# Matrix products that walk their columns backwards in blocks of sixteen

## The chip, the cores and the metric

One core of a Trainium2 chip runs the kernel. The metric is device time in microseconds (us); the kernel before takes 2259.56 us, the median of three runs (2258.78 to 2261.01).

## The reference

The reference is two transformer-like blocks in float32 over 256 tokens with 2048 features, with 256 context tokens beside them in the first. Cut to the parts that carry weights:

```
# first block
mod    = silu(c) @ w_mod + b_mod                    # 2048 -> 6 x 2048, also for c_ctx
hx, hc = modulate(rms_norm(x)), modulate(rms_norm(ctx))
z      = h @ w_in                                   # queries, two gates, values, and the rest
o      = hgrn2_chunk_scan(...)                      # both directions, state from the context
merged = sigmoid(ga) * (y_a @ w_pa) + sigmoid(gb) * (y_b @ w_pb)
x      = x + g1 * (merged @ w_o)
a, b   = split(modulate(rms_norm(x)) @ w_up, 2)     # 2 x 5632 columns
x      = x + g2 * ((silu(dwconv_grid(a)) * b) @ w_down)
# second block, on 16 meta tokens and the 256 tokens
proj   = rms_norm_2(h) @ w_in_2                     # eight parts of 1024 columns
mixed  = [stick-breaking attention, differential attention], gated
y      = mixed @ w_out_2
return (h + y)[:, N_META:]
```

Nearly all the work is products of an activation matrix of 256, 272 or 512 (tokens and context) columns with weights that are read once each.

## The kernel before, in words

Everything is kept features by tokens: 128 features on the partitions, tokens along the free axis. A product makes 128 output features: for each of its 16 (in "down": 11 per quarter) blocks of 128 input features it multiplies a 128x128 block of weights with 128 x T activations, and all of them add up in one bank of PSUM (`ACC`, four banks taken in turn).

For float32 accuracy, weights and activations are each split into a high and a low part of the type fp32r. ScalarE copies the weights that have landed in `RAW` to `HI` (line 488), VectorE writes the rest, raw minus high, to `LO` (line 1308), both in half products of 128 x 1024 values. TensorE then issues three matmuls for each block: high weights by high activations, high weights by low activations, low weights by high activations. Each matmul has its own load of 128 columns of weights (the LDWEIGHTS of the trace), which runs beside the matmul before it. All products go through `prod` (line 878) except the first three of "rec" (`early_step`, line 930) and the first two of "up" (`up_step`, line 1135), and all matmuls through `mm` at line 876.

The activations that stream through the array are `HX` (phases rec, mix and merge; in rec the token and the context stream are read by one matmul of 2 x 256 columns), `YAB` (merge), `MRG` (out), `HXU` (up), `SH` and `SL` (down), `U2` (attn: 272 columns where the 16 meta tokens take part, 256 where they don't) and `MIX` (proj). The core of `prod`, and the two-stream operand of rec:

```
o = out(k)
mm(o, HI[:, slot, k, 0:P], xh(k), start=first, stop=False)
mm(o, HI[:, slot, k, 0:P], xl(k), start=False, stop=False)
ins = mm(o, LO[:, slot, k, 0:P], xh(k), start=False, stop=last)

xch, xcl = (lambda k: HX[:, 0:3:2, k, 0:T]), (lambda k: HX[:, 1:4:2, k, 0:T])
```

The phases follow each other in the order mod1, rec, mix, merge, out, up, down, attn, proj, each a loop that is the same on all engines. Between the products stand TensorE's small matmuls of the recurrence (`mix_level` and others) and of the attention, into four other banks (`AUX`). SyncE fetches a weight block of 1 MB for every product into one of the four slots of `RAW`, as soon as VectorE has made the low part out of the block that was there. Order is kept by semaphores: `lo_half` says that half a product's weights are split, `mm_half` that half a product is computed, `bank_free` that a bank has been read.

In `HX`, `HXU`, `MRG`, `YAB`, `SH`, `SL` and `MIX` the 256 columns of one block lie beside each other, 1024 bytes on each partition; in `U2` a block has 320 columns, of which 272 are used. The two streams of `HX` lie 32 KB apart.

Of the kernel before, what the change touches and what calls it, by code (L numbers as in the profile page):

```python
# [14 lines left out]
P = 128  # L15
D = 2048
KD = D // P
T = 256
# [113 lines left out]
def build(nc, xct, metat, crow, vec, con1, con2, wts, wdown, park, outt):  # L132
    ctx = ExitStack()
    with ctx:
        base = 8320

        def at(name, kb, shape, dt=F32):
            return nc.alloc_sbuf_tensor_at(name, shape, dt, offset=base + int(kb * 1024))
# [6 lines left out]
        HI = at("hi", 32, [P, 2, 16, P], F32R)  # L145
        LO = at("lo", 49, [P, 2, 16, P], F32R)
# [19 lines left out]
        HXU = at("hxu", 66.1875, [P, 2, KD, T], F32R)  # L166
# [101 lines left out]
        ACC = ctx.enter_context(nc.psum_tensor("acc", [P, 4, 512], F32))  # L268
# [70 lines left out]
        def prod_index(ph, i, p):  # L339

            k = KINDS[ph]
            n = p - k[:p].count("m")
            return PROD0[ph] + i * (len(k) - k.count("m")) + n
# [5 lines left out]
        def used(ph, i, p):  # L349

            return 2 * (unit(ph, i, p)[0] - UNIT0["rec0"])

        def halves(ph):
            return ((0, DH), (DH, DT)) if ph == "down" else ((0, 8), (8, 16))
# [517 lines left out]
        def _(pe):  # L872
            for one in (kd_tr, v_tr, s_mm, o_mm, ss2_mm, ss3_mm, d_sc, dv_tr, d_av, b_z, bv_tr, b_av):
                pe.sem_inc(one, 1)
            def mm(*a, **k):
                return pe.matmul(*a, **k)  # L876

            def prod(ph, i, p, xh, xl, out, groups=None, bank_wait=None, between=None,
                     lo_at=None, inputs=None, each=1, needs=None):


                q, slot = prod_index(ph, i, p), prod_index(ph, 0, p) % 2
                if bank_wait is None:
                    pe.wait_ge(bank_free, q - 3)
                elif bank_wait is not False:
                    pe.wait_ge(bank_free, bank_wait)
                n = halves(ph)[1][1]
                for h, (a, b) in enumerate(halves(ph)):
                    if h and between:
                        between()  # L890
                    pe.wait_ge(lo_half, (used(ph, i, p) if lo_at is None else lo_at) + h + 1)
                    for k in range(a, b):
                        if needs and k in needs:
                            pe.wait_ge(inputs, needs[k])
                        elif inputs and not needs and k % 4 == 0:
                            pe.wait_ge(inputs, each * (k // 4 + 1))
                        first, last = groups(k) if groups else (k == 0, k == n - 1)
                        o = out(k)
                        mm(o, HI[:, slot, k, 0:P], xh(k), start=first, stop=False)
                        mm(o, HI[:, slot, k, 0:P], xl(k), start=False, stop=False)  # L900
                        ins = mm(o, LO[:, slot, k, 0:P], xh(k), start=False, stop=last)
                    ins.then_inc(mm_half, 1)

            def rows(i, p):
# [19 lines left out]
            xch, xcl = (lambda k: HX[:, 0:3:2, k, 0:T]), (lambda k: HX[:, 1:4:2, k, 0:T])  # L924
# [5 lines left out]
            def early_step(s, k, high, low):  # L930

                if k % 8 == 0:
                    pe.wait_ge(lo_half, 2 * s + k // 8 + 1)
                o = ACC[:, s, :].rearrange("p (s t) -> p s t", s=2)
                mm(o, high, xch(k), start=k == 0, stop=False)
                mm(o, high, xcl(k), start=False, stop=False)
                ins = mm(o, low, xch(k), start=False, stop=k == KD - 1)
                if k == KD - 1:
                    ins.then_inc(mm_half, 2)

# [23 lines left out]
            for k in range(KD - LAG, KD):  # L964
                early_step(2, k, HIV[:, k, :], LOV[:, k, :])

            def rec_turns(i):

                pe.wait_ge(kd_ready, i + 1)
                pe.wait_ge(kdt_ready, 1 + i)  # L970
                for d in range(2):
                    for t in range(2):
                        ins = pe.transpose(AUX[:, 0, (2 * d + t) * P:(2 * d + t + 1) * P], EXC[:, d, t * P:(t + 1) * P], c1("ident"))  # L973
                ins.then_inc(kd_tr, 1)
                pe.wait_ge(bank_free, prod_index("rec", i, 4) + 1)
                pe.wait_ge(vt_ready, 1 + i)
                for s in range(2):
                    for t in range(2):
                        ins = pe.transpose(AUX[:, 1, (2 * s + t) * P:(2 * s + t + 1) * P], VS[:, s, t * P:(t + 1) * P], c1("ident"))  # L979
                ins.then_inc(v_tr, 1)  # L980

            def rec_state(i):

                pe.wait_ge(kdt_ready, 1 + i + 1)
                pe.wait_ge(vt_ready, 1 + i + 1)
                pe.wait_ge(s_ready, 1 + i)
                for d in range(2):
                    for t in range(2):
                        ins = mm(AUX[:, 2, d * P:(d + 1) * P], KDT[:, 2 * d + t, :], VCT[:, t, :], start=t == 0, stop=t == 1)
                ins.then_inc(s_mm, 1)  # L990

            def rec_query(ph, i, p, between=None):

                prod(ph, i, p, lambda k: HX[:, 0, k, 0:T], lambda k: HX[:, 1, k, 0:T], lambda k: ACC[:, 3, 0:T],
                     between=between)
# [6 lines left out]
            def rec_head(i, second=False):  # L1002

                for p in range(3):
                    prod("rec", i, 2 * p, xch, xcl, lambda k: ACC[:, p, :].rearrange("p (s t) -> p s t", s=2),
                         between=first_turns if second and p == 0 else None)
                    if second and p == 0:
                        rec_state(0)
                rec_query("rec", i, 6, lambda: rec_turns(i))
                rec_state(i)  # L1010
# [51 lines left out]
            def mix_head(i, peeled):  # L1062

                xh, xl = (lambda k: HX[:, 0, k, 0:T]), (lambda k: HX[:, 1, k, 0:T])

                prod("mix", i, 0, xh, xl, lambda k: ACC[:, 0, 0:T], between=None if peeled else lambda: mix_level(i - 1, 7))
                if peeled:
                    pe.wait_ge(s_ready, 1 + HEADS)
                else:
                    mix_outputs(i - 1)  # L1070
                mix_same(i)
                mix_level(i, 0)
                prod("mix", i, 1, xh, xl, lambda k: ACC[:, 1, 0:T], between=lambda: mix_level(i, 1))
                if not peeled:
                    mix_turn(i - 1)
                mix_level(i, 2)
                prod("mix", i, 2, xh, xl, lambda k: ACC[:, 2, 0:T], between=lambda: mix_level(i, 3))
                mix_level(i, 4)
                prod("mix", i, 3, xh, xl, lambda k: ACC[:, 3, 0:T], between=lambda: mix_level(i, 5))
                mix_level(i, 6)  # L1080
# [54 lines left out]
            def up_step(p, k):  # L1135

                slot = prod_index("up", 0, p) % 2
                if k % 8 == 0:
                    pe.wait_ge(lo_half, used("up", 0, p) + k // 8 + 1)
                o = ACC[:, p, 0:T]  # L1140
                mm(o, HI[:, slot, k, 0:P], HXU[:, 0, k, 0:T], start=k == 0, stop=False)
                mm(o, HI[:, slot, k, 0:P], HXU[:, 1, k, 0:T], start=False, stop=False)
                return mm(o, LO[:, slot, k, 0:P], HXU[:, 0, k, 0:T], start=False, stop=k == KD - 1)

            pe.wait_ge(bank_free, prod_index("up", 0, 1) - 3)
            for n in range(KD + BEHIND):
                if n < KD:
# [4 lines left out]
                    ins = up_step(0, n)  # L1152
                    if n % 8 == 7:
                        ins.then_inc(mm_half, 1)
                if n >= BEHIND:
                    ins = up_step(1, n - BEHIND)
# [11 lines left out]
            with pe.Fori(0, ITERS["down"]) as i:  # L1168
                for jj in range(2):
                    for q in range(4):  # L1170
                        p = 4 * jj + q
                        u = prod_index("down", i, p)
                        if jj == 0:
# [3 lines left out]
                             bank_wait=u - 4 if q == 0 else False)  # L1177
# [13 lines left out]
            def attn_head(i, peeled):  # L1191

                def proj(p, meta, between=None, inputs=None, needs=None, bank_wait=None):

                    a = 0 if meta else NMETA
                    prod("attn", i, p, lambda k: U2[:, 0, k, a:TA], lambda k: U2[:, 1, k, a:TA],
                         lambda k: ACC[:, p % 4, 0:TA - a], between=between, inputs=inputs, needs=needs,
                         bank_wait=bank_wait)

                def tokens_major(src, bank):  # L1200

# [4 lines left out]
                if peeled:  # L1206
                    proj(0, False, between=last_squares, inputs=u2_ready, needs={k: k + 1 for k in range(KD)},
                         bank_wait=PROD0["attn"] - 4)
# [22 lines left out]
                for c in range(2):  # L1231
                    r = slice(64 * c, 64 * c + 64)
                    mm(AUX[:, c, 0:P + NMETA], DQK[r, 0, NMETA:NMETA + P], DQK[r, 1, 0:P + NMETA], start=True, stop=True)
                    ins = mm(AUX[:, c, P + NMETA:P + NMETA + TA], DQK[r, 0, NMETA + P:TA], DQK[r, 1, :], start=True, stop=True)
# [4 lines left out]
                for key, (a, q, w) in enumerate(SBQ):  # L1239
                    ins = mm(AUX[:, 1, a:a + w], SKF[:, key * P:(key + 1) * P], SQF[:, q:q + w], start=True, stop=True)  # L1240
# [44 lines left out]
            with pe.Fori(0, ITERS["proj"]) as i:  # L1285
                for p in range(4):
                    prod("proj", i, p, lambda k: MIX[:, 0, k, 0:T], lambda k: MIX[:, 1, k, 0:T], lambda k: ACC[:, p, 0:T],
                         inputs=mix_ready, needs=head_order if p == 0 else {KD: 0})
# [789 lines left out]
```

## Time and profile before

| | |
|---|---|
| median of three runs | 2259.56 us |
| profiled execution, span from first to last instruction | 2259.2 us |
| TensorE, matmuls | 2223.9 us, 98% |
| TensorE, weight loads | 2143.9 us, 95% |
| VectorE | 1633.3 us, 72% |
| ScalarE | 995.8 us, 44% |
| DMA | 475.73 MB, 211 GB/s on average |

For the profiled execution there is the span alone, and it lies 0.4 us under the median of the runs. A matmul's duration in the trace runs from its start to the end of its pipeline, so neighbours overlap; what tells the pace is the distance from one start to the next, or a stretch divided by the matmuls in it. "PE" rows are matmuls and "PEld" rows weight loads. One row of the windows view gives a stretch of time and for each engine its busy time and the number of instructions.

### The profile page before, as it was taken

What the parts mean: (1) busy time and instruction counts of PE and PEld (TensorE: products, weight loads), DVE (VectorE), ACT (ScalarE), POOL (GpSimd) and SP (SyncE); (2) the same over time, 40 slices, a digit from 0 to 9 for tenths busy, and PEclk for the clock granted to TensorE, in tenths of its full rate; (3) what the DMA queues carried; (4) which work ended last, traced back from release to release, by engine and by line L of the source; (5) the groups of instructions that cost most, each with busy time, mean ns of one, the idle gap of its engine ahead of it and who ended that gap; (6) DMA issues with size and microseconds to landing.
All of it is one profiled execution on the core that took longest, in us unless ns stands there. A gap on an engine that the chain in (4) does not pass through costs nothing.

```text
span 2259.2 us, 48355 instructions
## 1 busy us (share of the span) xinstructions
PE 2223.9 (98%) x18451; PEld 2143.9 (95%) x18451; DVE 1633.3 (72%) x2523; ACT 995.8 (44%) x1402; POOL 8.4 (0%) x18
## 2 busy tenths in 40 slices
PE   5999999999999999999999999999999999999999
PEld 4788888999999999999999999999999999999999
DVE  4465565899987666998888888875656766767764
ACT  4332222565543333454444444444445444444453
POOL 0000000000000000000000000000000000000000
PEclk8999999999999999999999999999999999999999
DMA  9955565444468766894555555556556444444443
GB/s 404 401 228 206 197 233 191 168 149 149 149 225 312 284 257 239 339 354 169 200 192 199 188 186 198 194 211 202 189 185 233 150 152 165 149 154 162 149 177 139
DMA packets 69519, 475.73 MB, mean 211 GB/s; under 512 B 7728, under 2 KB 9776, under 8 KB 18384
## 3 DMA queue, kind: packets, MB, share of 16 engines
q1 hardware_dynamic: 68688, 467.59, 56.1%
q0 software_dynamic: 768, 7.26, 0.9%
q8 instruction: 44, 0.72, 0.1%
q14 instruction: 19, 0.16, 0.0%
HBM read 469.58 MB, written 5.24 MB: 210 GB/s over the span
## 4 chain that ended last, share of the span: by engine, by line
PE 93%; DMA 4%; DVE 2%; ACT 1%; issue 0%; SPq 0%; DVEq 0%; ACTq 0%
PE acc L876 87%; PE aux L876 5%; DMA raw<-wts 4%; DVE lo L1308 1%; PE aux L1203 0%; DVE cv L1744 0%; DVE n L1688 0%; ACT hi L488 0%; PE aux L979 0%; PE aux L973 0%; DVE raw L1318 0%; DVE u L1772 0%; PE aux L1250 0%; DVE hxu L1325 0%; PE aux L1252 0%
## 5 line engine op out<-in xcount | busy, mean ns | idle before, releaser
L1308 DVE TENSOR_TENSOR lo<-raw,hi 128x1024 fp32r<-128x1024 f32 (+1 forms) x714 | 810.0, 1168 | 185.0 <-ACT hi L488 180.3
L488 ACT ACTIVATE hi<-raw 128x1024 fp32r<-128x1024 f32 (+1 forms) x714 | 693.8, 1012 | 299.9 <-PE acc L876 235.2
L876 PE MATMUL acc<-hx,hi 128*128 128x256 f32 (+1 forms) x3040 | 648.4, 311 | 1.3 <-DVE hx L1371 1.3
L876 PEld LDWEIGHTS acc<-hx,hi 128*128 128x128 f32 x3040 | 488.8, 189 | 37.1 <-issue 2.4
L876 PE MATMUL acc<-hxu,hi 128*128 128x256 f32 x2816 | 479.8, 276 | 0.5 <-DVE lo L1308 0.3
L876 PE MATMUL acc<-hx,lo 128*128 128x256 f32 (+1 forms) x1520 | 468.1, 308 | 0.0
L876 PEld LDWEIGHTS acc<-hxu,hi 128*128 128x128 f32 x2816 | 424.1, 188 | 1.6 <-DVE hxu L1325 1.1
L876 PE MATMUL acc<-hxu,lo 128*128 128x256 f32 x1408 | 388.7, 276 | 0.0
L876 PE MATMUL acc<-u,hi 128*128 128x272 f32 (+1 forms) x2048 | 381.6, 288 | 0.0
L876 PEld LDWEIGHTS acc<-u,hi 128*128 128x128 f32 x2048 | 318.1, 189 | 4.3 <-issue 2.5
L876 PEld LDWEIGHTS acc<-hx,lo 128*128 128x128 f32 x1520 | 287.9, 189 | 16.7
L876 PE MATMUL acc<-u,lo 128*128 128x256 f32 (+1 forms) x1024 | 291.1, 284 | 0.0
L876 PEld LDWEIGHTS acc<-hxu,lo 128*128 128x128 f32 x1408 | 264.3, 188 | 0.0
L876 PE MATMUL acc<-sh,hi 128*128 128x256 f32 x704 | 194.3, 276 | 0.0
L876 PE MATMUL acc<-sl,hi 128*128 128x256 f32 x704 | 194.3, 276 | 0.0
L876 PE MATMUL acc<-sh,lo 128*128 128x256 f32 x704 | 194.3, 276 | 0.0
L876 PEld LDWEIGHTS acc<-u,lo 128*128 128x128 f32 x1024 | 192.7, 188 | 0.0
L876 PEld LDWEIGHTS acc<-sh,hi 128*128 128x128 f32 x704 | 132.2, 188 | 0.0
L876 PEld LDWEIGHTS acc<-sl,hi 128*128 128x128 f32 x704 | 132.2, 188 | 0.0
L876 PEld LDWEIGHTS acc<-sh,lo 128*128 128x128 f32 x704 | 132.2, 188 | 0.0
L1744 DVE SCALAR_TENSOR_TENSOR cv<-at,vec,cv 128x256 f32<-128x256 f32 x308 | 129.5, 480 | 0.0
L876 PE MATMUL acc<-yab,hi 128*128 128x256 f32 x512 | 91.2, 281 | 0.3 <-DVE lo L1308 0.3
(301 smaller groups left out, 2327.0 us busy)
## 6 DMA issues: line engine op xcount, KB each, us to landing
raw<-wts SPq DMA_DIRECT2D x389, 1024.0 KB, 4.8
raw<-wdown SPq DMA_DIRECT2D x64, 704.0 KB, 4.1
xc<-xct SPq DMA_DIRECT2D x1, 4096.0 KB, 12.6
rawx<-wts SPq DMA_DIRECT2D x2, 1024.0 KB, 24.3
x<-xct SPq DMA_DIRECT2D x1, 2048.0 KB, 11.1
park<-x POOLq DMA_DIRECT2D x1, 2048.0 KB, 9.6
xf<-park POOLq DMA_DIRECT2D x1, 2048.0 KB, 9.0
outt<-outs SPq DMA_DIRECT2D x16, 128.0 KB, 3.4
```

Source lines behind the costliest of these rows:

```text
L488: A.activation(HI[:, slot, a:b, 0:P], RAW[:, p % 4, a:b, :], ACT.Copy).then_inc(hi_half, 1)
L876: return pe.matmul(*a, **k)
L1308: V.tensor_tensor(LO[:, slot, a:b, 0:P], RAW[:, p % 4, a:b, :], HI[:, slot, a:b, 0:P].bitcast(F32), ALU.subtract).then_inc(lo_half, 1)
L1744: mark(V.scalar_tensor_tensor(acc4[n % 2], a, w, acc4[n % 2], ALU.mult, ALU.add))
```

## The change

Each operand of the products, the columns read and the columns written in PSUM, gets an access pattern with another order. `paired` takes 256 columns as two halves of eight blocks of 16 and goes through them from the last block to the first, in each step first the block of the first half and then that of the second: columns 112 to 127, 240 to 255, 96 to 111, 224 to 239, and so on. `streams` does it with the two streams of rec: columns 240 to 255 of the one, 240 to 255 of the other, 224 to 239 of the one, and so on. Inside a block the columns ascend. The result of a column goes to the place where it went before. The products with 272 columns keep their order. Number, size and operands of the matmuls, waits, loads and all other engines' instructions stay as they are.

```
+            def paired(x):
+                return x.rearrange("p (b a c) -> p a b c", b=2, c=16)[:, ::-1]
+
+            def streams(x):
+                return x.rearrange("p s (a c) -> p a s c", c=16)[:, ::-1]
...
             def prod(ph, i, p, xh, xl, out, groups=None, bank_wait=None, between=None,
-                     lo_at=None, inputs=None, each=1, needs=None):
+                     lo_at=None, inputs=None, each=1, needs=None, order=paired):
...
-                        o = out(k)
-                        mm(o, HI[:, slot, k, 0:P], xh(k), start=first, stop=False)
-                        mm(o, HI[:, slot, k, 0:P], xl(k), start=False, stop=False)
-                        ins = mm(o, LO[:, slot, k, 0:P], xh(k), start=False, stop=last)
+                        o, high, low = order(out(k)), order(xh(k)), order(xl(k))
+                        mm(o, HI[:, slot, k, 0:P], high, start=first, stop=False)
+                        mm(o, HI[:, slot, k, 0:P], low, start=False, stop=False)
+                        ins = mm(o, LO[:, slot, k, 0:P], high, start=False, stop=last)
...
-                o = ACC[:, s, :].rearrange("p (s t) -> p s t", s=2)
-                mm(o, high, xch(k), start=k == 0, stop=False)
+                o = streams(ACC[:, s, :].rearrange("p (s t) -> p s t", s=2))
+                mm(o, high, streams(xch(k)), start=k == 0, stop=False)
...
                     prod("rec", i, 2 * p, xch, xcl, lambda k: ACC[:, p, :].rearrange("p (s t) -> p s t", s=2),
-                         between=first_turns if second and p == 0 else None)
+                         between=first_turns if second and p == 0 else None, order=streams)
...
-                o = ACC[:, p, 0:T]
-                mm(o, HI[:, slot, k, 0:P], HXU[:, 0, k, 0:T], start=k == 0, stop=False)
+                o, high, low = (paired(x) for x in (ACC[:, p, 0:T], HXU[:, 0, k, 0:T], HXU[:, 1, k, 0:T]))
+                mm(o, HI[:, slot, k, 0:P], high, start=k == 0, stop=False)
...
                          lambda k: ACC[:, p % 4, 0:TA - a], between=between, inputs=inputs, needs=needs,
-                         bank_wait=bank_wait)
+                         bank_wait=bank_wait, order=(lambda x: x) if meta else paired)
```

## Rows read from the trace of the kernel before

**Rows 1.** The page: busy time, share of the span and instructions of each engine.
```profile
PE 2223.9 (98%) x18451; PEld 2143.9 (95%) x18451; DVE 1633.3 (72%) x2523; ACT 995.8 (44%) x1402; POOL 8.4 (0%) x18
```
**Rows 2.** What TensorE waited for: us in total, times, longest.
```profile
PE aux L876 <- DMA raw<-wts: 21.4, 7, 16.5
PE acc L876 <- DMA raw<-wts: 7.1, 5, 4.9
```
**Rows 3.** Stretches in mix, merge, out, up, down, attn, proj: busy (instructions), clock, DMA share, GB/s.
```profile
core 0: us, PE busy (x) PEld busy (x) DVE busy (x) ACT busy (x) POOL busy (x), PEclk, DMA share, GB/s
410.00:650.00 240.00, 239.80 (x2069) 238.71 (x2068) 224.28 (x388) 141.04 (x247) 4.74 (x9) 1.00 0.43 157
660.00:900.00 240.00, 240.00 (x2040) 240.00 (x2040) 168.13 (x198) 93.69 (x112) 0.00 (x0) 1.00 0.74 280
930.00:990.00 60.00, 59.65 (x506) 59.45 (x505) 56.77 (x66) 26.63 (x33) 0.00 (x0) 1.00 0.99 386
1010.00:1490.00 480.00, 479.45 (x4217) 478.40 (x4217) 406.64 (x703) 228.34 (x317) 0.00 (x0) 1.00 0.53 189
1500.00:1730.00 230.00, 230.00 (x2032) 230.00 (x2031) 135.32 (x175) 107.33 (x153) 0.00 (x0) 1.00 0.61 206
1740.00:2160.00 420.00, 419.89 (x3366) 410.05 (x3366) 294.35 (x495) 198.66 (x289) 0.00 (x0) 1.00 0.43 155
2175.00:2255.00 80.00, 80.00 (x709) 80.00 (x708) 38.75 (x44) 28.73 (x27) 0.00 (x0) 1.00 0.47 169
```
**Rows 4.** Ten microseconds of merge, the same columns.
```profile
700.00:710.00 10.00, 10.00 (x88) 10.00 (x87) 9.17 (x11) 4.44 (x5) 0.00 (x0) 1.00 0.98 366
```
**Rows 5.** Groups of product matmuls, whole span: count, busy us, mean ns of one.
```profile
L876 PE MATMUL acc<-hxu,hi 128*128 128x256 f32 x2816 | 479.8, 276 | 0.5 <-DVE lo L1308 0.3
L876 PE MATMUL acc<-hx,hi 128*128 128x256 f32 x2304 | 414.0, 283 | 0.0
L876 PE MATMUL acc<-hx,hi 128*128 128x512 f32 x736 | 234.4, 400 | 1.3 <-DVE hx L1371 1.3
L876 PE MATMUL acc<-sh,hi 128*128 128x256 f32 x704 | 194.3, 276 | 0.0
L876 PE MATMUL acc<-u,hi 128*128 128x256 f32 x1024 | 185.1, 284 | 0.0
L876 PE MATMUL acc<-u,lo 128*128 128x256 f32 x512 | 142.8, 279 | 0.0
```
**Rows 6.** The third of each block's matmuls in mix and in merge.
```profile
L876 PE MATMUL acc<-hx,lo 128*128 128x256 f32 x543 | 151.3, 279 | 0.0
...
L876 PE MATMUL acc<-hx,lo 128*128 128x256 f32 x456 | 128.1, 281 | 0.0
```
**Rows 7.** Order of time, TensorE in rec: start us, us from there.
```profile
340.38 0.40 PE L876 MATMUL acc<-hx,lo 128*128 128x512 f32 x1
340.61 0.63 PE L876 MATMUL acc<-hx,hi 128*128 128x512 f32 x2
341.08 0.39 PE L876 MATMUL acc<-hx,lo 128*128 128x512 f32 x1
```
**Rows 8.** Order of time, small matmuls in mix, then in attn.
```profile
421.65 0.60 PE L876 MATMUL aux<-qla 128*128 128x128 f32 x4
...
1783.02 0.86 PE L876 MATMUL aux<-lz,con 128*128 128x416 f32 x2
1783.72 0.55 PE L876 MATMUL aux<-lz,onep 128*128 128x144 f32 x4
```
**Rows 9.** Waits in out (930 to 990 us), then in up (1100 to 1300 us).
```profile
ACT hi L488 <- DMA raw<-wts: 4.2, 9, 1.5
...
DVE cv L1730 <- ACT cv L754: 23.9, 18, 1.4
```

More of the change, by code:

```diff
@@ L933, in early_step @@
                     pe.wait_ge(lo_half, 2 * s + k // 8 + 1)
-                o = ACC[:, s, :].rearrange("p (s t) -> p s t", s=2)
-                mm(o, high, xch(k), start=k == 0, stop=False)
-                mm(o, high, xcl(k), start=False, stop=False)
-                ins = mm(o, low, xch(k), start=False, stop=k == KD - 1)
+                o = streams(ACC[:, s, :].rearrange("p (s t) -> p s t", s=2))
+                mm(o, high, streams(xch(k)), start=k == 0, stop=False)
+                mm(o, high, streams(xcl(k)), start=False, stop=False)
+                ins = mm(o, low, streams(xch(k)), start=False, stop=k == KD - 1)
                 if k == KD - 1:
@@ L1139, in up_step @@
                     pe.wait_ge(lo_half, used("up", 0, p) + k // 8 + 1)
-                o = ACC[:, p, 0:T]
-                mm(o, HI[:, slot, k, 0:P], HXU[:, 0, k, 0:T], start=k == 0, stop=False)
-                mm(o, HI[:, slot, k, 0:P], HXU[:, 1, k, 0:T], start=False, stop=False)
-                return mm(o, LO[:, slot, k, 0:P], HXU[:, 0, k, 0:T], start=False, stop=k == KD - 1)
+                o, high, low = (paired(x) for x in (ACC[:, p, 0:T], HXU[:, 0, k, 0:T], HXU[:, 1, k, 0:T]))
+                mm(o, HI[:, slot, k, 0:P], high, start=k == 0, stop=False)
+                mm(o, HI[:, slot, k, 0:P], low, start=False, stop=False)
+                return mm(o, LO[:, slot, k, 0:P], high, start=False, stop=k == KD - 1)
             pe.wait_ge(bank_free, prod_index("up", 0, 1) - 3)
```

## The prediction

> **What bounds the kernel now.** I read the busy line first: TensorE's matmuls fill 98% of the span [rows 1]. Then what TensorE waits for: 28.5 us for weights from DMA [rows 2], nearly all at the start, where nothing is changed (the slices of the page show the empty stretch there); all else together is under 4 us. So from the start of rec on, TensorE is the bound, and the time is the number of product matmuls times the distance from one to the next. Last I read that distance, stage by stage, out of stretches that hold nothing but products [rows 3]:
>
> - up 480/4217 = 113.8 ns and down 230/2032 = 113.2 ns; proj the same within its edges (80/709 = 112.8). I take 113.3 for all three.
> - merge 240/2040 = 117.6 ns; out 60/506 = 118.6 with 0.35 us idle, I take 117.6 as well.
> - rec, 512 columns: three matmuls in 341.08 - 340.38 = 0.70 us, 233 ns each [rows 7].
> - mix and attn mix both paces. A matmul at the slow pace lasts 281 ns (merge), at the fast one 276 (down) [rows 5, 6]; mix with 279 lies three fifths of the way up, near 116 ns. The 256-column matmuls of attn have 279 and 284 in their two groups [rows 5], where the first of a product counts longer, so again near 116.
>
> All of them run at a granted clock of 1.00, the level of 2.4 GHz. At one column per cycle 256 columns would need 106.7 ns and 512 columns 213.3. So each product matmul has an excess: 6.6 ns at the fast pace, 10.9 at the slow one, 20 with 512 columns.
>
> **Where the excess comes from decides everything.** Three things in the rows:
>
> 1. Merge and up have the same shapes and the same kind of operands, and yet two paces, each held for hundreds of microseconds [rows 3]. So at least 4.3 ns is no fixed cost of a matmul.
> 2. It is not the traffic of others: in ten microseconds of merge with the DMA engines 98% busy the pace is 88 matmuls in 10 us, just as over the whole stage at 74% [rows 3, 4], and down with VectorE at 59% runs as up at 85% [rows 3]. What is left is TensorE against itself: columns streaming in while the next weights load beside them (x2040 of both in 240 us).
> 3. The small matmuls show what a fixed cost can be. Four of 128 columns last 0.60 us in all, so with 0.275 for the last they start (0.60 - 0.275)/3 = 0.108 us apart, each with its own weights. Two of 416 columns start (1783.72 - 1783.02)/2 = 0.35 us apart [rows 8]; at half rate, two cycles a column, which fits, that is 346.7 ns and an excess of some 3. So where the columns come at half the rate, beside the same weight loads, excess is 1 to 3 ns.
>
> My reading: of the excess, 2 to 3 ns is fixed, and the rest is the full-rate column reads and the weight reads getting in each other's way in SBUF. How often they do depends on how their addresses run against each other, which explains why one shape can have two paces. The change alters just that: columns now go downwards through memory, and every 128 columns' worth of addresses takes as long as a load of 128 weight columns does. If weight loads walk from the last column to the first, the two move together and never meet. That direction no row shows, and it is the weak point.
>
> The Trainium skill ("TensorE: Matmul & The Clock Gate", Single matmul latency and Back-to-back issue gap) gives columns/2.4 + 2.5 ns for the distance of warm matmuls; that would be 109.2 and 215.8 here, and the trace is 4 to 18 ns above it. By this page alone the sum below is the same within 3 us.
>
> **The change part by part.** It adds no instruction, no byte and no wait. If the meetings go, I take 109 ns for 256 columns: a matmul can't follow faster than its weights, and 0.108 is the closest that any pair of load and matmul comes [rows 8]. For 512 columns 213.3 + 2.4 = 215.7. Counts are from the groups [rows 5]; with the third matmul they are half as many again as the group of high weights.
>
> - up 2816 x 1.5 = 4224, at 4.3 ns: 18.2 us
> - down 3 x 704 = 2112, at 4.3: 9.1 us
> - proj 4 blocks of four products of 48 = 768, at 4.3: 3.3 us
> - rec, 512 columns: 736 x 1.5 + 48 of the early third product = 1152, at 17.6: 20.3 us
> - rec, eight query products, 384 at about 7: 2.7 us
> - mix 4 x 8 x 48 = 1536 at 7: 10.8 us
> - merge, 48 products, 2304 at 8.6: 19.8 us
> - out 16 x 48 = 768 at 8.6: 6.6 us
> - attn, four products of a head without the meta tokens, 1024 x 1.5 = 1536 at 7: 10.8 us
> - attn with 272 columns, 1536: order unchanged, nothing.
>
> Sum 101.6 us. What is late next takes some back:
>
> - Out: DMA is 99% busy at 386 GB/s, and ScalarE already waits 4.2 us for weights [rows 3, 9]. Eight blocks of 1.05 MB per four products ask for 8.4 MB / 22.6 us = 371 GB/s now and 401 at the new pace. I leave 2 of the 6.6 us.
> - Mix: VectorE is busy 224 of 240 us [rows 3], and the stage would shrink to 230 with a chain of small matmuls in it. I leave half, 5.4.
> - Up: VectorE busy 407 of 480 us; it also waits 23.9 of 200 us for ScalarE's copy of a finished bank [rows 9], 1.3 us in each pair of products. That wait follows on the product's end, so it is slack, and 0.9 us of it is left when a pair takes 10.5 instead of 10.9. Nothing lost.
> - Merge (VectorE 70%, DMA 280 GB/s, 302 after), down, attn, proj: covered. One microsecond for chains in attn.
>
> 101.6 - 4.6 - 5.4 - 1 = 90.6, so 2259.2 - 90.6 = 2168.6 in the profiled execution, whose span is 0.4 us under the median: 2169 us.
>
> What the pattern itself costs, no row shows: 15 jumps in a matmul of 256 columns, 31 in one of 512. The nearest row is the 512-column matmul, which jumps once between two streams: 233 against twice 113.3 (excess 6.4 ns) or twice 117.6 (saving 2.2) [rows 3, 7]. So a jump lies between -2 and +6 ns. I take nothing, since 117.6 is the pace of the same tile HX. The upper end would be 13,632 x 15 x 6 ns, over a millisecond, and I hold it for very unlikely. The other rule against the change is in the Trainium skill ("SBUF — State Buffer", Door 1: The DMA port swizzle): any PSUM pattern that isn't contiguous slows matmuls significantly, PSUM having lines of 8 bytes. Runs of 64 bytes fill whole lines, so by the mechanism it names the cost would be nothing, by its letter it would be rival 3.
>
> **Rivals.**
>
> 1. *Only the slow pace goes.* The 113.3 has some other cause (a fixed cost at full rate), and only the meetings beyond it vanish. Then mix 1536 x 2.7, rec's queries 384 x 2.7, merge 2304 x 4.3, attn 1536 x 2.7, out nothing, and 512 columns 233.3 to 2 x 113.3 = 226.7, 1152 x 6.6: 4.1 + 1.0 + 9.9 + 4.1 + 7.6 = 27, to 2232 us. For it: 113.3 is steady over 900 us of three stages with different tiles. Against: the small matmuls' 1 to 3 ns.
> 2. *The order doesn't matter.* The excess depends on when a weight load starts, not on addresses: 2259.6, within 3 us. For it: the two paces appear with like tiles. The Trainium skill says ("TensorE: Matmul & The Clock Gate", Step-by-step: what each phase is for) that TensorE has two independent SBUF read ports and that loading weights takes no bandwidth from the running matmul; by it the columns' order could not matter, and the excess that the rows show would be left as it is.
> 3. *Every jump costs TensorE cycles*, on the read or the write. There are 13,632 x 15 + 1152 x 31 = 240,000 jumps. One cycle of 0.42 ns each is 100 us and just eats the whole gain of 102: that is the point from which it decides. Two cycles, with the meetings gone, give 2259 - 102 + 200 = 2357 us; one cycle without any gain 2360. For it: no product of this kernel has ever more than one jump. Against: the two-stream matmul of rec, with a jump, takes less than two of merge without one. A variant on the same side: weights are read upwards, and more meetings come than before; at one more of 6.6 ns in each matmul about +90 us.
>
> **Chances.** Forecast 0.50 (own range 2155 to 2200). Rival 1 0.14 (2215 to 2245). Rival 2 0.10. Rival 3 0.26, of which 0.08 lies near the break-even point, between 2264 and 2290, and the rest above. Faster by over 0.2% 0.64, within 0.2% (4.5 us, what runs of this kernel can tell) 0.10, slower 0.26. The range from 2150 to 2285 leaves out the costly part of rival 3, 0.18, and little below.
>
> **What would show it.** Right: down, up and proj at 109 ns (a stretch of 230 us with some 2110 instructions), merge at 109 too, one pace instead of two, 512 columns at 216, the mean of one near 272; TensorE still 98% busy; more idle time of TensorE in out, ended by the split of weights or DMA. Rival 1: 113.3 everywhere and 276 ns. Rival 2: both paces in the same places. Rival 3: product matmuls over 118 ns, 272-column ones in attn as long as now. My forecast is wrong if 256-column products still start 113 ns or more apart in down.

## The result: slower, and one pace in place of two

The changed kernel takes 2286.93 us, the median of four runs (2285.32 to 2287.49), against 2259.17 for the kernel before (2249.98 to 2261.01): ratio 1.0132, interval 1.0108 to 1.0156. Forecast were 2169 us in a range from 2150 to 2285, and slower with a chance of 0.26. The profiled execution has a span of 2285.5 us, 26.3 more than before. The kernel before does not always take the same time: one of its four runs here lies near 2250, and experiment 7 comes back to that.

The page after, TensorE and its waits, beside [rows 1, 2]:

```profile
PE 2247.8 (98%) x18451; PEld 2174.1 (95%) x18451; DVE 1633.1 (71%) x2523; ACT 995.5 (44%) x1402; POOL 8.4 (0%) x18
```
```profile
PE aux L876 <- DMA raw<-wts: 23.0, 8, 17.2
PE acc L876 <- DMA raw<-wts: 8.9, 7, 3.8
```

The stages after, as in [rows 3, 4] (each stage begins a little later, so attn and proj are taken 20 us later):

```profile
core 0: us, PE busy (x) PEld busy (x) DVE busy (x) ACT busy (x) POOL busy (x), PEclk, DMA share, GB/s
410.00:650.00 240.00, 239.87 (x2055) 239.25 (x2054) 223.32 (x386) 141.15 (x246) 4.21 (x8) 1.00 0.43 153
660.00:900.00 240.00, 240.00 (x2048) 240.00 (x2047) 166.74 (x194) 95.53 (x115) 0.00 (x0) 1.00 0.76 281
930.00:990.00 60.00, 59.77 (x510) 59.57 (x509) 56.62 (x67) 26.43 (x33) 0.00 (x0) 1.00 0.98 378
1010.00:1490.00 480.00, 479.90 (x4087) 479.63 (x4087) 393.82 (x682) 218.43 (x300) 0.00 (x0) 1.00 0.51 183
1500.00:1730.00 230.00, 230.00 (x1962) 230.00 (x1961) 133.16 (x174) 99.91 (x136) 1.70 (x2) 1.00 0.57 194
1760.00:2180.00 420.00, 419.89 (x3344) 410.08 (x3343) 291.95 (x491) 197.48 (x288) 0.00 (x0) 1.00 0.43 154
2195.00:2275.00 80.00, 80.00 (x684) 80.00 (x683) 41.07 (x47) 30.75 (x30) 0.00 (x0) 1.00 0.49 167
```

Divide stretch by matmuls (a row also counts the two or three that lie only partly in the stretch, which matters in short stretches): up 480/4087 = 117.4 ns, down 230/1962 = 117.2, proj 117.0, merge 240/2048 = 117.2, out 117.6. Where there were 113.3 and 117.7 there is one pace now, 117.3, and it is nearly the slow one. Rec alone gained, beside [rows 7]: three matmuls in 341.32 - 340.64 = 0.68 us, 226.7 ns instead of 233.3.

```profile
340.64 0.39 PE L876 MATMUL acc<-hx,lo 128*128 128x512 f32 x1
340.87 0.61 PE L876 MATMUL acc<-hx,hi 128*128 128x512 f32 x2
341.32 0.39 PE L876 MATMUL acc<-hx,lo 128*128 128x512 f32 x1
```

The groups say the same in durations, beside [rows 5]: 276 has become 280 in up, and 400 has become 393 in rec.

```profile
L876 PE MATMUL acc<-hxu,hi 128*128 128x256 f32 x2816 | 496.4, 280 | 0.2
L876 PE MATMUL acc<-hx,hi 128*128 128x512 f32 x736 | 229.9, 393 | 1.4 <-DVE hx L1379 1.4
```

The account: up, down and proj 7104 x 4.0 = +28.4 us; mix 2069 x (116.8 - 116.0) = +1.7; attn 3366 x (125.6 - 124.8) = +2.7; merge and out 3072 x -0.3 = -0.9; rec 1152 x -6.67 = -7.7; waits for the first weights +3.4. Together +27.6, measured +26.3.

### The profile page after: what moved, and what is told of

Its sections match the earlier page's. It is cut to its first block, busy times and chain, and to the rows that moved or that the text cites. A ratio compares the mean times of both kernels' runs of the same rounds, so it can differ in the third digit from the quotient of the medians.

```text
span 2285.5 us, 48355 instructions
## 1 busy us (share of the span) xinstructions
PE 2247.8 (98%) x18451; PEld 2174.1 (95%) x18451; DVE 1633.1 (71%) x2523; ACT 995.5 (44%) x1402; POOL 8.4 (0%) x18
## 4 chain that ended last, share of the span: by engine, by line
PE 93%; DMA 4%; DVE 1%; issue 0%; ACT 0%; SPq 0%; DVEq 0%; ACTq 0%
PE acc L876 88%; PE aux L876 5%; DMA raw<-wts 4%; DVE lo L1316 0%; PE aux L1211 0%; DVE n L1696 0%; PE aux L981 0%; PE aux L987 0%; DVE raw L1326 0%; DVE u L1780 0%; ACT hi L488 0%; PE aux L1258 0%; DVE hxu L1333 0%; SPq L374 0%; PE aux L1067 0%
## 5 line engine op out<-in xcount | busy, mean ns | idle before, releaser
L876 PE MATMUL acc<-hxu,hi 128*128 128x256 f32 x2816 | 496.4, 280 | 0.2
L876 PEld LDWEIGHTS acc<-hxu,hi 128*128 128x128 f32 x2816 | 429.8, 188 | 0.9 <-DVE hxu L1333 0.8
L876 PE MATMUL acc<-hxu,lo 128*128 128x256 f32 x1408 | 393.7, 280 | 0.0
## 6 DMA issues: line engine op xcount, KB each, us to landing
xc<-xct SPq DMA_DIRECT2D x1, 4096.0 KB, 13.4
```

## The experiments

In the edits `-` is the changed kernel unless said otherwise. "Pace" is the distance from one matmul's start to the next. In the runs with TensorE alone it is the mean over the second half of a case or more, worked out from the start times in the trace. "First column" or "at 48" is the place of the columns against the weights, in columns of 4 bytes, within the 512 bytes that one block of weights takes on a partition; in the kernel it is 48 for most tiles. The runs of a changed version were taken beside the kernel before, and their ratios are to it; only `rec_only` and `paired_only` ran beside each other, as did `near_weights` and `ahead56`, `low_moved` and `low_moved_rec`.

**1. The change in rec alone** (`rec_only`) and **in the 256-column products alone** (`paired_only`).

```
# rec_only
-                     lo_at=None, inputs=None, each=1, needs=None, order=paired):
+                     lo_at=None, inputs=None, each=1, needs=None, order=lambda x: x):
...
# paired_only, in streams(x)
-                return x.rearrange("p s (a c) -> p a s c", c=16)[:, ::-1]
+                return x
```

> The change in the two-stream products of rec alone; all 256-column products read plainly as before. Theory A (each form of product has its own pace, set by its own reading order): 1152 matmuls of 512 columns at 226.7 ns instead of 233.3, 7.7 us faster than before, about 2251; 256-column stages as before (113.3 in up, down and proj, 117.6 in merge and out). Rival L (the pace of a stage is carried over from what ran ahead of it, so that rec's order decides the pace of the later stages too): up and down at another pace than 113.3 although their order is the old one.

Measured: 2252.27 us, the median of ten runs, ratio 0.9977 (0.9959 to 0.9995), span 2250.2. Six runs lie at 2251 to 2253, one at 2244 and three near 2280. Rec gained its 7.7 us, and merge and down kept their paces, as theory A has it. But out, whose instructions and order are those of the kernel before, ran at 113.3: 443 matmuls in this stretch, where the kernel before has 422. And up began at 117.8 and changed to 113.3 after some 30 us. So theory A holds for rec only; a stage can change its pace although nothing in it was changed, which is on the side of rival L.

```profile
935.00:985.00 50.00, 50.00 (x443) 50.00 (x443) 49.16 (x57) 22.31 (x28) 0.00 (x0) 1.00 0.98 391
```

> The change in the 256-column products alone; rec's two-stream products read plainly. Theory A: 117.3 ns in every 256-column product, 233.3 in rec, so 7.7 us slower than the whole change, about 2295. Rival L: the 256-column stages go back to 113.3 and 117.6, about 2259.

Measured: 2309.41, ratio 1.0236 (1.0210 to 1.0263). Both numbers missed. Merge has 117.2, but up 480/4003 = 119.9 and down 230/1919 = 119.9:

```profile
660.00:900.00 240.00, 240.00 (x2048) 240.00 (x2047) 169.00 (x200) 94.66 (x113) 0.00 (x0) 1.00 0.75 280
1030.00:1510.00 480.00, 480.00 (x4003) 480.00 (x4002) 384.95 (x672) 212.71 (x293) 0.00 (x0) 1.00 0.51 182
1530.00:1760.00 230.00, 230.00 (x1919) 230.00 (x1918) 125.69 (x158) 96.33 (x130) 0.00 (x0) 1.00 0.58 191
```

So the parts don't add up: in the kernel the paired order has two paces at the same addresses, 117.4 and 120.0. Which one out, up and down get differs between this kernel and the changed one, though only rec's order, earlier on, differs; merge, between them, has 117.4 in both. By start times the 120.0 begins in out and ends in attn, and proj has 117.4 again.

**2. TensorE alone** (`bench1`): weights loaded beside columns as in the kernel, no other engine busy.

> Products alone, not the reference's computation: only TensorE works, with 96 matmuls for each of some 60 cases, as in the kernel two blocks of weights (high, low) in turn against two tiles of columns. The cases differ in the order in which columns are read and written, in the first column (which moves the columns' addresses against the weights' in steps of 64 bytes), in the number of columns, and in what ran ahead. With nothing else on the chip's memories, the plain order at the kernel's distance of 48 columns should give 113.3 or 117.8 ns if the excess is TensorE's own (every theory here), about 109 if it comes from other engines. Theory M (columns and weights meet in SBUF): pace depends on the first column, in some order reaches about 109; only the reading order counts, so reading paired and writing plainly gives 117.3, reading plainly and writing paired 113.3 or 117.8. Theory J (a jump costs time): paired, paired upwards and blocks from the end are alike at any first column, 8-column blocks (31 jumps) cost twice as much over the floor as 16, 32-column blocks half. Theory P (PSUM): writing paired and reading plainly gives 117.3, the reverse 113.3. The plain cases after fillers of different length show two paces if the pace depends on the start.

Four cases at the kernel's distance of 48 columns, eight microseconds of each: plain, paired, read paired and written plainly, read plainly and written paired. The counts include the two or three matmuls that reach in from outside, so the pace is not 8 us divided by them; 70 or 71 stand for some 117 to 118 ns, 73 for 113.

```profile
core 0: us, PE busy (x) PEld busy (x) ACT busy (x) POOL busy (x), PEclk, DMA share, GB/s
82.00:90.00 8.00, 8.00 (x70) 8.00 (x69) 0.00 (x0) 0.00 (x0) 1.00 0.00 0
173.50:181.50 8.00, 8.00 (x71) 8.00 (x70) 0.00 (x0) 0.00 (x0) 1.00 0.00 0
406.00:414.00 8.00, 8.00 (x70) 8.00 (x69) 0.00 (x0) 0.00 (x0) 1.00 0.01 2
417.00:425.00 8.00, 8.00 (x73) 8.00 (x72) 0.00 (x0) 0.00 (x0) 1.00 0.00 0
```

By start times, in ns:

```
first column          0      16     32     48     64     80     96     112
plain                 120.0  117.8  120.0  117.8  120.0  117.8  120.0  117.8
paired                121.4  113.3  116.7  117.4  120.8  116.7  116.7  117.4
paired, upwards       120.0         120.0         120.0         120.0
blocks from the end   117.8         120.0         117.8         120.0
                        first column 0    first column 48
read paired, write plain    120.7             117.4
read plain, write paired    120.0             113.3
halves swapped (1 jump)     120.0             117.8
paired in eights (31 jumps) 133.3             120.0
paired in 32s (7 jumps)     120.0             118.6
two streams: plain          226.7             233.4
two streams: down as changed 233.4            226.7
two streams: up             240.0             240.0
plain at 48 after matmuls of 24, 40, 56, 72, 104, 136 columns: 117.8 117.8 113.3 117.8 113.3 117.8
plain at 48 by columns: 128 to 224: 111.7;  240: 113.3;  272: 123.3;  288: 133.4;  320: 146.7
```

Four things follow. The excess is TensorE's own: 113.3, 117.8, 117.4, 226.7 and 233.4 come up with nothing else running. It is made on the reading side: reading paired gives the paired pace however it is written, and writing paired leaves plain's two paces (113.3 is one of them). Jumps between blocks of 16 columns have no cost of their own: paired at 16, with 15 of them, runs at 113.3, the lowest pace that any order has. Shorter blocks may cost: in eights, with 31 jumps, the pace is 13 ns over plain at one place and 2 at another. The place of the columns against the weights counts, as theory M said: at 0 the two-stream products are faster plain (226.7) than downwards (233.4), at 48 it is the other way round. But nothing reaches 109.

**3. Starts, places and widths** (`bench2`).

> Products alone again, not the reference's computation: TensorE only, 48 matmuls a case, 96 cases. What the first such run left open: (1) Is the excess tied to the weight load or to the columns? With 352 to 512 columns in one run of addresses a weight load covers less and less of a matmul: theory W (each weight load costs the column reads a few stretches of 16 columns) expects a constant excess of 13 to 20 ns over columns / 2.4, theory C (reading at full rate costs one part in sixteen) expects 6.25%, 9 ns at 352 and 13 ns at 512. (2) Is the pace of an order its own or does it depend on the start? Paired at distances 0, 16 and 48 after eight fillers: theory S (start matters only for the plain order, which crosses the weights; paired moves along with them) expects one pace per distance, 113.3 at 16 and 117.4 at 48; rival T expects two or more paces as for the plain order. (3) Is there an order or distance at 109? If columns and weights that move together could keep clear of each other, one of the eight distances of the two-stream order should reach 216 and one of the paired ones 109; if the least cost of a weight load is one stretch of 16 columns, nothing falls under 113.3 and 220.

```
plain at 48, columns:       352    384    416    448    480    512
pace                        160.0  173.4  186.7  202.3  216.1  233.3
over columns / 2.4           13.4   13.4   13.4   15.6   16.1   20.0
paired at 0, eight starts:   120.7 to 120.9
paired at 16, eight starts:  113.3 twice, 116.5 to 116.7 six times
paired at 48, eight starts:  117.0 to 117.6
two streams down, eight first columns: 233.2 228.3 228.4 226.7 233.2 228.3 228.4 226.7
```

From 352 to 416 columns the excess stands at 13.4 ns (and 13.4 at 320): it does not grow with the columns as theory C has it, which speaks for theory W, though at 448 to 512 it grows. Every matmul here has a weight load of its own, so a fixed cost of the matmul is not told apart from one of the load. Paired at 48 has one pace within 0.6 ns, at 16 two. Of the 96 cases none is under 113.3, nor under 226.6 with 512 columns.

**4. The starting matmul** (`bench3`).

> Products alone, not the reference's computation: TensorE only, plain order at the kernel's distance of 48 columns, 48 matmuls a case, each after one matmul of 8 to 256 columns; first one after another, then each from a case that followed a matmul of 56 columns. Theory S: both paces come up, 113.3 and 117.8, each steady within its case, by the length of the matmul ahead. If the pace before also matters, the two sweeps differ. At the end the paired order after 16 to 256 columns: 117.3 for all if its pace does not hang on the start, or 120.0 in some, as it had in up and down when rec ran plainly.

Plain after matmuls of 8 to 256 columns: 113.3 in 12 of 32 cases, 117.8 in 20, nothing between. With another case in front of each, the lengths that give 113.3 are partly others: 88 gave it only in the first sweep, 80 only in the second, and 56, repeated 32 times, gives now the one pace and now the other. So the length ahead does not choose the pace alone; what else does, within the exact timing of the start, no run shows. Paired: 117.0 to 117.6 in all 16; the 120.0 of `paired_only` did not come up.

**5. In the kernel: the place of the weights, and a matmul ahead** (`near_weights`, `ahead56`).

```
# near_weights
-        HI = at("hi", 32, [P, 2, 16, P], F32R)
-        LO = at("lo", 49, [P, 2, 16, P], F32R)
+        HI = at("hi", 32.125, [P, 2, 16, P], F32R)
+        LO = at("lo", 49.125, [P, 2, 16, P], F32R)
...
# ahead56, against rec_only, in prod
+                        if ahead and k == 0:
+                            mm(o[:, 0:ahead], HI[:, slot, k, 0:P], high[:, 0:ahead], start=True, stop=True)
```

> The changed kernel with the weight tiles HI and LO moved up by 128 bytes, so that the columns of HX, HXU, SH, MRG, YAB and MIX stand 16 columns from the weights' place in a 512-byte row instead of 48; nothing else differs. Theory M (how addresses of columns and weights stand to each other sets the pace): in TensorE's run alone, paired order at 16 had two paces, 113.3 and 116.7, and 117.3 at 48; so up, down (its low tile at another distance), proj and merge at 113 to 117, rec's 512 columns at 228 to 233 instead of 226.7; in all 2287 - 13632 x 0.7 to 4.0 + 1152 x 2 to 6.7, that is 2240 to 2285. Rival J (15 jumps cost a fixed time, wherever the tiles lie): 117.3 in all stages, 2287.

Measured: 2274.34, ratio 1.0063 (1.0028 to 1.0098): nearly 13 us less than the changed kernel by nothing but the tiles' addresses. Theory M; a fixed price of a jump would have left 2287. Up runs at 480/4114 = 116.7:

```profile
1010.00:1490.00 480.00, 480.00 (x4114) 479.75 (x4113) 395.47 (x688) 218.18 (x300) 0.00 (x0) 1.00 0.52 184
```

> The change in rec's two-stream products alone, all others plain, and one matmul of 56 columns more ahead of the first product of every round of merge and of out (nine in all), written where the product overwrites it. Theory S (the plain order has two paces at the same addresses, held from how the stream of matmuls started; a short matmul ahead can switch it): merge and out switch from 117.8 to 113.3, 3072 x 4.4 = 13.5 us less than with rec's change alone, about 2238. Rival U (the pace belongs to the stage: its tiles, its DMA traffic): merge and out stay at 117.8, 2252.

Measured: 2250.83, ratio 1.0006 (0.9959 to 1.0052), not the 2238 expected. The pace did switch within merge, but not as wished: one stretch came to 113.3 by start times (20 us with 178 matmuls, those at its edges included), another stayed slow (40 us with 342):

```profile
660.00:700.00 40.00, 40.00 (x342) 40.00 (x342) 34.43 (x38) 15.63 (x19) 0.00 (x0) 1.00 0.92 341
770.00:790.00 20.00, 20.00 (x178) 20.00 (x178) 14.31 (x20) 7.75 (x9) 0.00 (x0) 1.00 0.70 260
```

That both paces stand in one stage with one code speaks against rival U. The kernel before shows it too: its out is at 117.8 but for some 5 us from 924 us on, at 113.3. As a remedy the matmul ahead failed, and experiment 4 shows why: after 56 columns either pace can come. Nor was 2238 the right mark, since out was fast in `rec_only` already.

**6. An order or a place with one good pace** (`bench4`).

> Products alone, not the reference's computation: TensorE only, 48 matmuls a case, in search of an order with one pace at 113.3 from every start. Eight reading orders at distances 16 and 48, each after matmuls of 8, 32, 48 and 96 columns; the plain order with the low weights moved by 64, 128 and 256 bytes; the plain order at distances that split the 64-byte stretches. Theory S (where column and weight reads meet is a matter of phase, and an order can offer one stable phase or several): each order has its own set of one or two paces; the plain one 113.3 and 117.8 by start, and at least one other may have 113.3 alone. Rival R (113.3 is only ever one of two phases): every order that shows 113.3 after one start shows 117 or more after another. Orders with 3, 7 or 15 jumps have the plain paces among theirs if a jump is free.

```
after matmuls of             8      32     48     96 columns
plain, 48                    113.3  117.8  117.8  113.3
blocks of 64, 48             113.4  117.8  117.7  113.4
blocks of 32, 16             117.8  117.7  113.3  113.3
blocks of 16, 16             120.0  120.0  120.0  120.0
plain, low weights + 64 B    118.3  118.3  118.4  118.3
plain, low weights + 128 B   113.4  113.4  113.3  113.4
plain, low weights + 256 B   117.8  117.7  113.3  113.3
```

No order had 113.3 from all four starts: rival R for the orders. But a place has: with the low weights 128 bytes higher, the plain order runs at 113.3 from every start.

**7. That place in the kernel** (`low_moved`, `low_moved_rec`).

```
# against the kernel before (low_moved) and against rec_only (low_moved_rec)
-        LO = at("lo", 49, [P, 2, 16, P], F32R)
+        LO = at("lo", 49.125, [P, 2, 16, P], F32R)
```

> The kernel before with one number changed: the tile of low weights LO starts 128 bytes higher, so that high and low weights stand 48 and 16 columns from the columns read. Theory S (pace is the phase in which column and weight reads meet; where the low weights lie decides which phases are stable): as in TensorE's run alone, 113.3 ns from every start, so merge, out, mix and attn lose their 117.8: 3072 x 4.4 + 1536 x 2.7 + 1536 x 2.5 = 21 us less than the 2259 of the profiled run before, 2238 in every run, instead of values from 2249 to 2286. Rec unchanged. Rival U (a stage's pace comes from its tiles or its other traffic): merge at 117.8 as before, 2259 give or take.

Measured: 2244.13 (2242.92 to 2245.80 in 12 runs), ratio 0.9961 (0.9940 to 0.9983). Merge has 230/2029 = 113.4 and down 210/1855 = 113.2; the third row is mix:

```profile
660.00:890.00 230.00, 230.00 (x2029) 229.89 (x2029) 165.57 (x192) 94.37 (x114) 0.00 (x0) 1.00 0.78 290
1500.00:1710.00 210.00, 210.00 (x1855) 210.00 (x1854) 122.57 (x155) 94.47 (x128) 0.00 (x0) 1.00 0.59 194
410.00:650.00 240.00, 239.48 (x2069) 236.76 (x2068) 223.87 (x388) 142.08 (x247) 4.73 (x9) 1.00 0.44 153
```

The kernel before, beside it, gave 2248 to 2287 in 23 runs, 16 of them near 2249 and the others near 2258, 2276 and 2286; the version with the low weights moved spans 3 us. Against the 16 the gain is 5 us, against the profiled run before, one near 2259, it is 16. No run before of another cluster was profiled, so what sets the clusters apart is not shown. The span is 2243.1, 16.1 under before, where 21 were expected. By start times merge and attn gave nearly what was asked of them (9.5 and 3.2 us). Mix gave nothing: its row has the 2069 matmuls in 240 us of the kernel before [rows 3]. Out gave 0.6 of 3.4 us: its products start 113.3 ns apart, and there TensorE waits 1.2 us for the split of weights, before 0.3. Rec, expected unchanged, went from 233.3 to 231.8, some 2 us.

> The same with the change's order in rec's two-stream products. Theory S: 256-column products at 113.3 throughout; rec at 226.7 if its pace holds with the low weights at another distance, then 1152 x 6.6 = 7.6 us less than low_moved, 2230; if not, up to 233 and no gain.

Measured: 2242.83, ratio 0.9953 (0.9931 to 0.9976). Rec did not keep 226.7 beside the moved weights, it has 231.1 by start times, against 231.8 in `low_moved`; the gain over that is a microsecond, within the spread.

**8. The paired order with the low weights moved** (`paired_low_moved`, `bench5`).

> The changed kernel with the low weights LO 128 bytes higher, as in low_moved; nothing else. Theory S (what counts is how columns, high and low weights lie to each other): the paired order gets another pace than 117.3 in up and down, and it need not be 113.3, since the order that is best at one distance was not at another; a value between 2255 and 2290. Rival O (the paired order has 117.3 of its own, the place of the low weights does not matter for it): 2287 as the changed kernel.

Measured: 2298.67 (2291.86 to 2306.32), ratio 1.018 (1.0131 to 1.0229): above the range given, and all four runs lie above those of the changed kernel. Two are near 2292 and two near 2306; the profiled one is of the upper pair. Merge has 2040 matmuls in 240 us, where the changed kernel has 2048 (117.8 and 117.4 by start times), and up 470/3919 = 119.9:

```profile
660.00:900.00 240.00, 240.00 (x2040) 240.00 (x2039) 166.64 (x193) 94.24 (x114) 0.00 (x0) 1.00 0.76 280
1030.00:1500.00 470.00, 470.00 (x3919) 470.00 (x3918) 376.91 (x659) 209.68 (x288) 0.00 (x0) 1.00 0.51 182
```

> Products alone, not the reference's computation: TensorE only, 48 matmuls a case, distance 48, the low weights moved by 0, 64, 128... elements' bytes (0, 128, 256 and 384 bytes), each order after four different starts. Theory S: plain with 128 bytes has 113.3 from all starts, as before; paired has other paces with 128 than with 0; of the two-stream orders one may keep 226.7 with the low weights moved, which would tell the order to use in rec. Rival O: paired at 117.3 with all four places.

```
low weights moved by        0                128 B
paired, 48, four starts     117.0 to 117.6   117.8 to 117.9
plain                       113.3 or 117.8   113.3 to 113.4
two streams, plain          233.3 to 233.5   231.7 to 231.8
two streams, down           226.7            231.1 to 231.2
two streams, up             240.0            240.0
```

One and the same move of one tile helps the plain order, costs the paired one half a nanosecond, and takes most of the gain of rec's order away: of 6.7 ns between plain and downwards 0.6 are left. Moved by 256 bytes the low weights give the paces of 0 again, by 384 bytes those of 128. The 120 in up is no effect of the move, since `paired_only` has it without; the runs with TensorE alone don't show it for the paired order at 48.

## Why the prediction was wrong, step by step

- *TensorE bounds the kernel, and time is count times pace.* Right, before and after; the account closes within 1.3 us.
- *The excess is TensorE's own, not other engines' traffic.* Right, shown in experiment 2.
- *Of the excess, 2 to 3 ns is fixed and the rest is meetings of column and weight reads.* The mechanism holds so far: reading order, place and start each change the pace. The size was wrong. I took the floor from small matmuls that read columns at half rate and carried it over to reads at full rate. There each matmul with its load has an excess of 13.4 ns from 320 to 416 columns, and with 256 columns it was never under 6.6 in over 300 cases.
- *If columns and weights both go downwards, they never meet, so 109.* This is the step that failed. In which direction the weights are read no run shows. At the kernel's place the paired order has 117.0 to 117.6 alone and 117.4 or 120.0 in the kernel, all worse than the plain order's good pace, by 4.0 ns in the changed kernel. Up, down and proj had been in that good one (7104 matmuls, +28.4 us in place of -30.6). Two streams taken downwards had 226.7 at best and 233.2 at another place, where never meeting would have given 216.
- *Merge and out gain 8.6 ns each.* It was 0.3, from one pace to the other that lies close to it.
- *Rec gains 17.6 ns per matmul of 512.* It was 6.6, with `rec_only` the same. That it was a gain at all was luck of the place: at first column 0 the same order costs 6.7 ns.
- *The traffic of others is not the cause: 88 matmuls in 10 us of merge.* Right in what it says, but so short a stretch tells little, as the two or three matmuls at its edges make more than the 4 ns in question; experiment 2 is what shows it.
- *A jump costs nothing.* Right for blocks of 16 columns; with blocks of eight and four columns paces of 120.0 to 133.3 came up. Rival 3's mechanism is not the cause, though its side won. What came near is the variant named under it, other meetings than before, at 4 ns instead of 6.6 and only where the pace had been good.
- *The cover (VectorE in mix, DMA in out).* Not tested by the change, as nothing got faster there. `low_moved` bears it out as far as it goes: with products at 113.3 mix gained nothing and out 0.6 us, less than I had left them, while merge kept nearly all of its gain with DMA at 78%. That VectorE and DMA were the cause is not shown.
- The rule of the Trainium skill ("TensorE: Matmul & The Clock Gate", Step-by-step: what each phase is for) that loading weights takes nothing from the running matmul does not hold here: moving the low weights by 128 bytes, and nothing else, turns 117.8 into 113.3 ns.
- The rule of the Trainium skill ("SBUF — State Buffer", Door 1: The DMA port swizzle) that a PSUM pattern which isn't contiguous slows matmuls did not show: runs of 16 columns were written at 113.3.

A misreading helped the error along: I took 113.3 and 117.6 for more and fewer meetings of one smooth cost and 109 for where the scale ends. They are two paces in which one stream of instructions can settle, and the profile before held both.

What stays open: what makes the paces, and whether it lies in the memory; in which direction weights are read (two streams upwards cost 240.0, downwards 226.7 to 233.4 by place, but the plain order reaches 226.7 too); and why the paired order has 120 in up in two kernels but in no run of TensorE alone at that place.

## What to carry to other kernels

Where matmuls of up to some 300 float32 columns alternate with weight loads, look at the distance between their starts in long stretches: two values for one shape mean that the stream can settle in more than one pace, and a tile moved by 128 bytes can be worth more than another order of reading. Test such a thing with TensorE alone, from several starts, before a kernel is changed; and take a floor only from matmuls that read at the same rate. Where the runs of one kernel lie in clusters, compare clusters, not medians: the change costs 28 us against one cluster, 37 against the lowest and nothing against the highest, which seven of 64 later runs of the kernel before were in (2285 to 2287).

## What the runs showed of the hardware that was not expected

- The same product stream has two steady paces, 113.3 and 117.8 ns, by how it started: one matmul ahead of 32 different lengths gave the first pace 12 times and the second 20 times, and one length gave both. In the kernel a pace mostly holds for hundreds of microseconds, but it also changes within a stage.
- The order of writing PSUM in runs of 16 columns is free; the order of reading is worth 240.0 against 226.7 ns for 512 columns, and which order is best depends on the place of the columns against the weights.
- That place counts in steps that repeat after 256 bytes: first column 64 has the paces of 0, and low weights moved by 384 bytes those of 128 bytes.
- With 128 to 224 columns the pace is 111.6 to 111.7 ns whatever the width. It looks like that of the weight loads, but the small matmuls of [rows 8] start 108 ns apart with loads as wide.
- With one weight tile 128 bytes higher, a kernel whose runs lay between 2248 and 2287 us took 2243 to 2246 in all of twelve.
